# Squared ReLU of an MLP on VectorE in one operation instead of two ScalarE passes, in a decoder layer with seven-product matrix multiplications

## The reference

```
h2 = rms_norm(x, pre_mlp_norm_w[layer])
a = jax.nn.relu(jnp.einsum("bsd,df->bsf", h2, w_ff1[layer]))
m_out = jnp.einsum("bsf,fd->bsd", a * a, w_ff2[layer])
x = x + rms_norm(m_out, post_mlp_norm_w[layer])
```

## Time and profile before

| | |
|---|---|
| median of 3 runs | 2312.2 us (2311.11 to 2315.84) |
| the profiled execution's own time | 2307.1 us |
| its span in the trace | 2305.3 us |
| mean granted TensorE clock, share of full speed | 0.965 |

### The profile page before, as it was taken

The page is one execution under the profiler, slowest core; times in us unless marked ns, Lnnn a source line. Parts: engine busy times, 40 slices in busy tenths (PEclk is TensorE's granted clock), DMA queues, the critical chain, the costliest instruction groups (busy, mean ns, idle before and its releaser), DMA issues. The chain is left out here.

```text
span 2305.3 us, 27088 instructions
## 1 busy us (share of the span) xinstructions
PE 2125.1 (92%) x10177; PEld 1768.2 (77%) x10177; DVE 1528.3 (66%) x1922; ACT 891.7 (39%) x1504; POOL 546.5 (24%) x304
## 2 busy tenths in 40 slices
PE   6899999999989989659999859999979999999998
PEld 3688978878978778538887748777768888888887
DVE  6799999798066666456777667777736345544276
ACT  5423324233344434434444454444523133133153
POOL 4111112112111131232333312333225312700012
PEclk7999999999999989879999989999989999999999
DMA  5011212112365665434444464444666653643466
GB/s 184 19 55 55 85 35 78 51 55 66 128 200 191 207 200 179 167 120 151 141 136 137 139 228 150 131 134 139 201 222 211 237 205 143 227 170 114 148 228 217
DMA packets 252497, 339.19 MB, mean 147 GB/s; under 512 B 11536, under 2 KB 196112, under 8 KB 238544
## 3 DMA queue, kind: packets, MB, share of 16 engines
q1 hardware_dynamic: 218320, 316.29, 41.0%
q10 hardware_dynamic: 33728, 21.04, 2.9%
q0 software_dynamic: 320, 0.13, 0.0%
HBM read 226.14 MB, written 111.28 MB: 146 GB/s over the span
## 5 line engine op out<-in xcount | busy, mean ns | idle before, releaser
L1547 PE MATMUL psum<-x_hi_P,w_hi_P 128*128 128x512 f32 x896 | 353.9, 395 | 72.9 <-DVE x_lo_P L1492 58.5
L1741 PE MATMUL psum<-w_hi,hid_hi 128*128 128x512 f32 x896 | 349.7, 390 | 14.9 <-ACT hid_hi L1635 14.7
L1547 PE MATMUL psum<-x_lo_P,w_hi_P 128*128 128x512 f32 x896 | 351.1, 392 | 0.0
L1547 PE MATMUL psum<-x_hi_P,w_lo_P 128*128 128x512 f32 x896 | 350.7, 391 | 0.0
L1741 PE MATMUL psum<-w_lo,hid_hi 128*128 128x512 f32 x896 | 349.4, 390 | 0.0
L1741 PE MATMUL psum<-w_hi,hid_lo 128*128 128x512 f32 x896 | 349.3, 390 | 0.0
L597 DVE SCALAR_TENSOR_TENSOR c_buf<-u_buf,par_a,c_buf 128x1024 f32<-128x1024 f32 x240 | 342.9, 1430 | 8.5 <-ACT c_buf L445 1.3
L1476 DVE TENSOR_TENSOR w_lo_P<-w_raw,w_hi_P 128x512 fp32r<-128x512 f32 x224 | 213.6, 965 | 176.7 <-ACT w_hi_P L1472 176.5
L1640 DVE TENSOR_TENSOR hid_lo<-hid_raw,hid_hi 128x1024 fp32r<-128x1024 f32 x112 | 176.9, 1616 | 216.2 <-ACT hid_hi L1635 216.2
L1463 POOL TENSOR_TENSOR w_raw<-w_raw 128x512 f32<-128x512 f32 x128 | 201.0, 1590 | 459.4 <-DMA w_raw<-in_w 406.6
L1547 PEld LDWEIGHTS psum<-x_hi_P,w_hi_P 128*128 128x128 f32 x896 | 169.6, 189 | 119.2 <-issue 83.6
(11 more groups left out here) (231 smaller groups left out, 3934.4 us busy)
## 6 DMA issues: line engine op xcount, KB each, us to landing
scratch_hid<-stage SPq DMA_DIRECT2D x224, 256.0 KB, 3.5
hid_raw<-scratch_hid SPq DMA_DIRECT2D x56, 1024.0 KB, 4.8
w_raw<-in_w SPq DMA_DIRECT2D x52, 1024.0 KB, 6.1
w_grain<-in_w SPq DMA_DIRECT2D x48, 512.0 KB, 5.3
x_raw_P<-scratch_h2s SPq DMA_DIRECT2D x14, 1024.0 KB, 12.0
w_raw<-in_w_in SPq DMA_DIRECT2D x25, 512.0 KB, 3.9
scratch_h2s<-h2s SPq DMA_DIRECT2D x8, 1280.0 KB, 7.3
scratch_qk<-qout ACTq DMA_DIRECT2D x16, 512.0 KB, 2.9
```

The source lines that it names most:

```text
L1547: mm = nc.tensor.matmul(psum[:, bank_1(op, g), :], l, r, start=kt == 0 and i == 0, stop=kt == 3 and i == 2)
L1741: mm = nc.tensor.matmul(psum[:, bank, :], l, r, start=f == 0 and k == 0, stop=f == NFP - 1 and k == 2)
```

## The change

`relu_square` moves from the ScalarE list to the VectorE list and becomes one instruction, max(x, 0) times x. The semaphore `relu` goes. C11 is squared in slot 3, ahead of the weight split P3 and of `combine`; C21 in slot 7, ahead of the weight split P5; C22 and C12 in slot 1 of the next group, ahead of the weight split P1. The waits that ScalarE had ahead of the C11 square (for stores of two groups earlier, and at g = 0 for two events of phase_b) go with it. The last `late_squares` stands ahead of the last `combine`.

```diff
     def scalar(act):
-        def relu_square(buf, name, c, g, out):
-            act.wait_ge(sem["gather"], gathered(c, g))
-            nc.scalar.activation(buf[:], buf[:], ACT.Relu).then_inc(sem["relu"], 1)
-            act.wait_ge(sem["relu"], squared(name, g))
-            nc.scalar.activation(out, buf[:], ACT.Square).then_inc(sem["sq"], 1)
...
                 nc.scalar.activation(c_1[:], ps1("P1", g), ACT.Copy).then_inc(sem["copy"], 1)
-                if g >= 1:
-                    late_squares(g - 1)
             if g + 1 < NGRP:
                 high_w1(act, OPS[s - 1], g + 1)
-            if s == 3:
-                if g == 0:
...
-                if g >= 2:
-                    act.wait_ge(sem["hid_out"][g % 2], 16 * 7 * (g // 2))
-                relu_square(c_11, "11", "C11", g, quad("P1", g))
-            if s == 7:
-                relu_square(c_21, "21", "C21", g, c_21[:])
...
+        def relu_square(buf, c, g, out):
+            dve.wait_ge(sem["gather"], gathered(c, g))
+            nc.vector.scalar_tensor_tensor(out=out, in0=buf[:], scalar=0.0, in1=buf[:], op0=ALU.max,
+                                           op1=ALU.mult).then_inc(sem["sq"], 1)
+
+        def late_squares(g):
+            relu_square(c_7, "C22", g, quad("P4", g))
+            relu_square(c_x, "C12", g, quad("P2", g))
...
+            if s == 1 and g >= 1:
+                late_squares(g - 1)
             if s == 2:
                 gather("C11", c_11, c_1, "P2", g)
+            if s == 3:
+                if g == 0:
...
+                if g >= 2:
+                    dve.wait_ge(sem["hid_out"][g % 2], 16 * 7 * (g // 2))
+                relu_square(c_11, "C11", g, quad("P1", g))
...
                 gather("C12", c_x, c_x, "P3", g)
+                relu_square(c_21, "C21", g, c_21[:])
             if g + 1 < NGRP:
                 low_w1(dve, OPS[s - 1], g + 1)
...
             low_w2(dve, "P1", f)
+        late_squares(NGRP - 1)
         combine(NGRP - 1)
```

More of the change, by code:

```diff
@@ L1768, in slot @@
                 nc.scalar.activation(c_1[:], ps1("P1", g), ACT.Copy).then_inc(sem["copy"], 1)
-                if g >= 1:
-                    late_squares(g - 1)
             if g + 1 < NGRP:
                 high_w1(act, OPS[s - 1], g + 1)
-            if s == 3:
-                if g == 0:
-                    for b in range(2):
-                        act.wait_ge(sem["xn_out"][b], 16 * NCH // 2)
-                    act.wait_ge(sem["h2_t"], 2 * NCH)
-                if g >= 2:
-                    act.wait_ge(sem["hid_out"][g % 2], 16 * 7 * (g // 2))
-                relu_square(c_11, "11", "C11", g, quad("P1", g))
-            if s == 7:
-                relu_square(c_21, "21", "C21", g, c_21[:])
             if (g, s) in x_later:
                 high_x(act, x_later[(g, s)], 1)
-        def late_squares(g):
-            relu_square(c_7, "22", "C22", g, quad("P4", g))
-            relu_square(c_x, "12", "C12", g, quad("P2", g))
         def final_norm(i):
@@ L1816, in scalar @@
                             high_hid(act, 0, h)
-        late_squares(NGRP - 1)
         for f in range(3 * PIECE, NFP):
@@ L1864, in slot @@
                 low_x(dve, x_first[(g, s)], 0)
+            if s == 1 and g >= 1:
+                late_squares(g - 1)
             if s == 2:
                 gather("C11", c_11, c_1, "P2", g)
+            if s == 3:
+                if g == 0:
+                    for b in range(2):
+                        dve.wait_ge(sem["xn_out"][b], 16 * NCH // 2)
+                    dve.wait_ge(sem["h2_t"], 2 * NCH)
+                if g >= 2:
+                    dve.wait_ge(sem["hid_out"][g % 2], 16 * 7 * (g // 2))
+                relu_square(c_11, "C11", g, quad("P1", g))
             if s == 4:
@@ L1962 @@
              "wo_scale",
-             "w1_in", "w1_t", "w1_hi", "w1_lo", "xs_hi", "xs_lo", "st1", "copy", "gather", "relu", "sq", "comb",
+             "w1_in", "w1_t", "w1_hi", "w1_lo", "xs_hi", "xs_lo", "st1", "copy", "gather", "sq", "comb",
              "w2_t", "w2_hi", "w2_lo", "w2_free", "hid_hi", "hid_lo", "st2", "rd2", "wpost", "eps_c",
```

## The result

The changed kernel takes 2333.58 us (median of 4 runs, 2330.12 to 2335.02), the kernel before 2311.65 (4 runs, 2309.52 to 2315.84). The ratio is 1.0088, 95% interval 1.0075 to 1.0100: slower by 22 us (17 to 23). Forecast: 2332.

The account below looks back on a forecast made before the run. Stage 1 was taken to be bound by a loop of stores, weight load, splits and `combine`, slightly slower than TensorE. 17.1 + 2.4 + 0.6 = 20.1 us gave 2327.2, with the median's 5.1 us offset 2332 us; range 2322 to 2352.

Parts of the forecast that it names:

- The ring: Stage 1's loop of stores, weight load, weight splits and `combine`: 20.13 us a round, against 19.3 us of TensorE work.
- The price of the C11 square: Slot 3, between splits P2 and P3: the square lengthens each round by one fast VectorE operation, 0.61 us.
- the turn: VectorE operations with two SBUF inputs alternate with GpSimd's four subtractions after the weights land; 1.70 us each.
- rival 1: C11's square, both inputs one tile, hides beside GpSimd's work: only 3.1 us, 2315 us; chance 0.11.
- rival 2: L1855 still finds GpSimd busy, so each round pays up to 1.70 us: 50.7 us, 2363 us; chance 0.06.
- rival 3: Squares with two float32 SBUF sources run at half throughput, 1.22 us each: 40 us, 2352 us; chance 0.03.
- rival 4: ScalarE, rid of 256 passes, starts an awaited weight copy earlier; would need over 4.6 us; chance 0.03.
- The 28 rounds: Stage 1, 14 store rounds in each of two blocks, each longer by C11's 0.61 us: 17.1 us.
- The turn of the blocks: Between stage 1's two blocks VectorE is almost fully busy, so all four squares of that group count: 2.4 us.
- The end: End of stage 1: loads wait for the last weight split, behind one more C21 square: 0.6 us.
- the cover: Last stores of stage 1 queue behind 4 MB of weights, hiding the other squares: 0, or 2.5 us if gone.
- The first group: Start of stage 1, g = 0: C11's square delays token splits by 0.6 us at most.

## Why the prediction was right

**The ring and its bound.** As forecast: rounds of SyncE's stores set stage 1. Cutting the ring left 3.5 us of the cost, taking the one square out of it 2.3 or 1.6.

**The price of the C11 square, 0.61 us.** In the round shown it is 0.59. Both rivals about it fell by the trace. Reading one tile as both inputs does not spare the turn (1.78 us in the square's row), so rival 1 is out. A fifth operation does not find GpSimd busy: L1840 was at 0.68, and the doubled square cost 16.7 us, not 48, so rival 2 is out.

**Half throughput (rival 3).** The durations of the C21 squares, outside GpSimd's time, min/median/max ns, and those of the former L1855:

```profile
L1826 DVE SCALAR_TENSOR_TENSOR c<-c x32: 684/685/686, 1031.7 to 1712.8; 128x512 f32<-128x512 f32 x32
L1840 DVE TENSOR_TENSOR stage<-c,stage x32: 677/679/685, 1040.9 to 1717.0; 128x512 f32<-128x512 f32 x32
```

0.685 us against 0.679 for a plain two-input operation. So rival 3 is out as well. The rule that I cited from the Trainium skill, Vector Engine (DVE) Microarchitecture Reference, "Points that are easy to get wrong", does not hold for this instruction; the measurement decides.

**ScalarE's relief (rival 4).** With C11 behind `combine` ScalarE has lost all 256 passes, and the ratio is 1.0011. It pays nothing.

**The 28 rounds, 17.1 us.** In the two profiled executions the 28 rounds grew by 21.8 us (12.6 and 9.2 in the two blocks). Summed over them, the stretch from the start of split P1 (the first L1476 behind the landing) to the next stores grew by 17.5 us, from 8.39 to 9.01 a round: this is the forecast term, at 0.63 us a square. The stretch from the issue of the weight load (L1448) to the start of split P1 grew by 4.1 us, from 6.77 to 6.91 a round, and the issue of the stores by 0.2. The 4.1 us are a term that I had put at nothing. The clearest case: the load issued at 1091.91 us in the changed kernel was used only at 1099.17, 7.3 us later against 5.95 in the earlier trace rows, and that round took 22.04 us. In the ring such a delay counts in full. The same mean in the other traces is 6.83 us with C11 alone on VectorE, 6.90 with C11 twice and 6.83 with the other three twice; it is 6.79 with C11 on ScalarE and 6.74 with C11 behind `combine`. So the four kernels with the square in the ring lie 0.1 us above the three without, near 3 us over 28 rounds. These are single traces, and the single rounds of the kernel before lie anywhere from 6.2 to 7.8; whether the longer ring makes landings later, and how, is not shown.

**The turn of the blocks, 2.4 us.** Measured between stores: 45.90 us against 43.47, so 2.43. VectorE is busy 25.83 of 26 us there (columns as in the earlier trace rows; the second row belongs to the end of stage 1):

```profile
1360.00:1386.00 26.00, 19.39 (x66) 14.43 (x65) 25.83 (x28) 13.70 (x17) 7.58 (x4) 0.82 0.39 144
1690.00:1700.00 10.00, 6.70 (x30) 5.22 (x28) 9.96 (x17) 6.58 (x12) 0.00 (x0) 1.00 1.02 380
```

**The end, 0.6 us, the rest covered by the full DMA engines.** The second row shows them full again (1.02). The last two stores of stage 1 are 12.05 us apart instead of 9.44, 2.6 more, and then take 9.16 us to issue instead of 11.67. From the one start to the other end that is 21.21 us against 21.11: the cover held. From the stores at 1679.73 to the first matmul of stage 2 (1709.92) it was 30.2 us, 1.3 less than before, where I had forecast 0.6 more. Over all ten traces this time lies between 30.2 and 31.6, so no cost of 0.6 us can be told here.

**The first group, where I had put at most 0.6 us.** This was too little by about a microsecond. The first stores came 2.05 us later, of which the first weight load of that stretch (1002.09 against 1001.56), behind phases that the change does not touch, accounts for 0.5. VectorE's rows in the changed kernel:

```profile
1033.54 1.78 DVE L1826 SCALAR_TENSOR_TENSOR stage<-c_x 128x512 f32<-128x512 f32 x1
1035.25 1.78 DVE L1476 TENSOR_TENSOR w_lo_P<-w_raw,w_hi_P 128x512 fp32r<-128x512 f32 x1
```

The square of C12 meets GpSimd here, takes a turn, and split P1 starts without any idle time before it. The step that failed here is the one that gave the first group only the C11 square of g = 0, as if C21, C22 and C12 always lay in idle time.

**The sum** of 20.1 us stands against 22 by the medians; the difference is within the interval of the ratio, 17 to 23 us. Some of this closeness is luck. The two profiled executions differ by 26.4 us: 0.5 ahead of stage 1, 1.5 in the first group, 21.8 in the rounds, 2.4 at the turn, 1.3 less at the end, and 1.4 more in stage 2, which I had called unchanged. From the first stores to the first matmul of stage 2 it was 23.0 us, where I had forecast 20. And I had added 5.1 us to 2327.2 because the profiled execution of the kernel before lay that far under its median. That of the changed kernel, 2333.51, lies on its median. So the mechanism and the price of a square are borne out round by round, and the total only as closely as executions of one kernel agree.

## What to carry to other kernels

An engine that is busy 66% can lie on the path that sets the time without a row that says so: look for a round that is longer than TensorE's own, and follow one turn of it through the queue order of the DMA issuer. An operation costs what it adds between the last wait and the signal that the ring needs; the same operation behind that signal was next to free here, 1.6 us against 22 for the whole change. Before trading instructions between engines, try the order of the DMA queue: a load that stood behind stores was worth 36 us, more than all squares together.

## What the runs showed of the hardware that I had not expected

A VectorE operation with the same tile as both of its SBUF inputs waits for GpSimd as one with two tiles does: 1.78 us in GpSimd's time, 0.685 outside it. And the number of such slow operations is set by GpSimd's list, not by VectorE's: with four, five or six VectorE operations of this kind from the landing to the first operation of `combine` (the kernel before, the changed one, the one with C11 twice), four were slow, as many as GpSimd has subtractions, and each further one cost about 0.6 us. With the other three squares twice, four in a row were slow in the first group too, at other places of the list (1039.40 to 1046.27 us).
